# Layer 0 first, the modulation whole inside it, the context inside layer 1, its projections behind the attention part

## What is computed

```python
def first_block(x, p, positions, ...):                 # two layers
    cos, sin = rotary_tables(positions, x.dtype)
    h = x
    for i in range(DEPTH):                             # DEPTH = 2
        hn = rmsnorm(h, norm1[i])
        z = hn @ w_in[i]                               # pool part u, q, k, v
        ...                                            # rotary on q and k
        pool_out = pool_mixer(u, pool_w[i], pool_scale[i])
        attn_out = dilated_mixer(q, k, v)              # 12 heads of 64
        h = h + concat([pool_out, attn_out]) @ w_out[i]
        hn = rmsnorm(h, norm2[i])
        h = h + square(relu(hn @ w_up[i])) @ w_down[i] # 1024 -> 4096 -> 1024
        gate = sigmoid(rmsnorm(h, norm3[i]) @ w_gate[i])
        h = h + gate * (p[i] @ w_ple[i])
    return rmsnorm(h, final_norm)

def second_block(x, c, ctx, c_ctx, w_mod, b_mod, ...): # one layer
    mod = silu(c) @ w_mod + b_mod                      # w_mod is 1024 x 6144
    mod_c = silu(c_ctx) @ w_mod + b_mod
    ...
    h = modulate(x, norm1_g, sh1, sc1)
    hc = modulate(ctx, norm1_g, csh1, csc1)            # ctx: 256 context tokens
    ...
    # gated delta rule, 4 heads of 128, both directions: the context's final
    # state is the latent's first; of the context only k, v, beta and g count
    o_ctx, o_lat = bidir_gated_delta(dn_ctx, dn_lat)
    mix = branch_merge(h, o_lat, ...)                  # three branches and w_o
    x = x + g1 * mix
    x = x + g2 * swiglu(modulate(x, norm2_g, sh2, sc2), w_ffn_in, w_ffn_out)
    return rmsnorm(x, final_g)
```

## Time and profile before

| | |
|---|---|
| median of 3 runs | 1499.83 us |
| the profiled execution: its span, its own time | 1493.0 us, 1494.76 us |
| busy on PE, DVE, ACT, POOL | 1354.7, 902.5, 701.3, 134.1 us |
| prelude | 0 to 222.2 us |
| layer 0, layer 1 | 222.2 to 571.3 us, 574.2 to 929.8 us |
| latent part | 930 to 1493 us |
| read from HBM | 216.26 MB |

### The profile page before, as it was taken

The page is one execution under the profiler, slowest core; times in us unless marked ns, Lnnn a source line. Parts: engine busy times, 40 slices in busy tenths (PEclk is TensorE's granted clock), DMA queues, the critical chain, the costliest instruction groups (busy, mean ns, idle before and its releaser), DMA issues.

```text
span 1493.0 us, 26105 instructions
## 1 busy us (share of the span) xinstructions
PE 1354.7 (91%) x10476; PEld 1282.4 (86%) x10476; DVE 902.5 (60%) x1265; ACT 701.3 (47%) x1025; POOL 134.1 (9%) x110
## 2 busy tenths in 40 slices
PE   2896889979999988979999998898889999999997
PEld 2775779869999987968999998898778999899997
DVE  2867867755555467675555458756755556554553
ACT  3754544545444445464444445654424454534442
POOL 0025011120000010130000004001520000000000
PEclk9988999989999999979999999899999999999999
DMA  8742634325555553523555544344200555455550
GB/s 298 226 141 86 206 113 142 114 85 167 172 170 182 176 187 105 163 76 114 169 170 184 200 157 138 113 142 142 85 1 29 170 191 166 141 181 189 178 169 29
DMA packets 175843, 219.04 MB, mean 147 GB/s; under 512 B 5001, under 2 KB 159463, under 8 KB 175591
## 3 DMA queue, kind: packets, MB, share of 16 engines
q1 hardware_dynamic: 173986, 212.80, 43.8%
q10 hardware_dynamic: 1732, 4.52, 0.8%
HBM read 216.26 MB, written 1.05 MB: 146 GB/s over the span
## 4 chain that ended last, share of the span: by engine, by line
PE 74%; DVE 12%; DVEq 4%; issue 4%; ACT 3%; DMA 1%; ACTq 0%; SPq 0%
PE bank L629 21%; PE bank L631 20%; PE bank L630 20%; DVE w_lo L620 2%; PE bank L1359 2%; PE bank L870 1%; PE bank L858 1%; DMA w_raw<-in_w_mod 1%; DVE arena L1174 1%; ACT w_hi L611 1%; PE bank L1540 1%; PE bank L1422 1%; DVE arena L2200 1%; PE bank L1341 1%; DVEq L2160 1%
## 5 line engine op out<-in xcount | busy, mean ns | idle before, releaser
L620 DVE TENSOR_TENSOR w_lo<-w_raw,w_hi 128x1024 fp32r<-128x1024 f32 (+1 forms) x406 | 491.5, 1252 | 178.0 <-ACT w_hi L611 170.2
L629 PE MATMUL bank<-act_hi,w_hi 128*128 128x256 f32 x1808 | 522.0, 289 | 29.7 <-DVE act_lo L2123 11.1
L630 PE MATMUL bank<-act_lo,w_hi 128*128 128x256 f32 x1808 | 517.1, 286 | 0.0
L631 PE MATMUL bank<-act_hi,w_lo 128*128 128x256 f32 x1808 | 516.8, 286 | 0.0
L611 ACT ACTIVATE w_hi<-w_raw 128x1024 fp32r<-128x1024 f32 (+1 forms) x406 | 405.0, 1041 | 168.2 <-PE bank L631 112.8
L629 PEld LDWEIGHTS bank<-act_hi,w_hi 128*128 128x128 f32 x1808 | 352.8, 195 | 36.5 <-issue 12.7
L630 PEld LDWEIGHTS bank<-act_lo,w_hi 128*128 128x128 f32 x1808 | 352.8, 195 | 0.3 <-issue 0.2
L631 PEld LDWEIGHTS bank<-act_hi,w_lo 128*128 128x128 f32 x1808 | 352.6, 195 | 0.0
L629 PE MATMUL bank<-side_hi,w_hi 128*128 128x256 f32 x896 | 258.9, 289 | 6.7 <-DVE w_lo L620 6.7
L630 PE MATMUL bank<-side_lo,w_hi 128*128 128x256 f32 x896 | 254.8, 284 | 0.0
L631 PE MATMUL bank<-side_hi,w_lo 128*128 128x256 f32 x896 | 254.8, 284 | 0.0
(11 more groups left out here) (315 smaller groups left out, 1510.2 us busy)
## 6 DMA issues: line engine op xcount, KB each, us to landing
w_raw<-in_w_in SPq DMA_DIRECT2D x40, 1024.0 KB, 5.6
w_raw<-in_w_up SPq DMA_DIRECT2D x32, 1024.0 KB, 5.6
w_raw<-in_w_down SPq DMA_DIRECT2D x32, 1024.0 KB, 5.4
w_raw<-in_w_mod SPq DMA_DIRECT2D x24, 1024.0 KB, 5.2
w_raw<-in_w_ffn_in SPq DMA_DIRECT2D x22, 1024.0 KB, 5.1
w_raw<-in_w_gate SPq DMA_DIRECT2D x20, 1024.0 KB, 5.1
w_raw<-in_w_ffn_out SPq DMA_DIRECT2D x11, 1024.0 KB, 4.9
w_raw<-in_w_out SPq DMA_DIRECT2D x8, 1024.0 KB, 5.0
```

The costliest lines, as they stand in the source:

```text
L620: nc.vector.tensor_tensor(wlo[:, slot, 0:n], raw[:, l % RAW, n * half:n * (half + 1)], whi[:, slot, 0:n].bitcast(F32), ALU.subtract).then_ ...
L629: nc.tensor.matmul(o, ahi, bhi, start=start, stop=False, skip_group_check=True)
L630: nc.tensor.matmul(o, ahi, blo, start=False, stop=False, skip_group_check=True)
L631: return nc.tensor.matmul(o, alo, bhi, start=False, stop=stop, skip_group_check=True)
```

## The change

The prelude is gone, and the layers are written out one after the other instead of as a loop.

- Layer 0 starts as soon as the vectors and `x` are in. Its normed input is made straight from the PSUM banks with the transposed `x`.
- The modulation goes whole into layer 0. `w_mod` is cut in 24 chunks of 512 rows by 512 columns, and nothing is split: PE reads the loaded chunk itself as the fp32 moving operand, with 32 stationary columns (`mod_cond`, tile `silu_c_cols`, of which two hold numbers and the rest zeros). The four row tiles of a chunk write to four groups of 32 partitions of one bank. One pair of chunks fills a bank. ACT copies it (`modr`), `mod_columns` sums the groups and turns them into columns, and DVE adds the offsets (`modc`). Twelve chunks stand between the transposes and products of the attention part, twelve behind the down steps of the feed-forward part, one to every third step from step 16 on (`ATT_EXTRA`, `FFN_EXTRA`).
- The context goes into layer 1. ACT scales its rows in the q and k part, PE transposes them behind step 4, ACT makes the modulated `hc`. Behind the last V stand its four projections, unsplit too (`project_whole`: 16 fp32 matmuls of 256 columns a chunk), its `ba` product and the convolution. Then comes its delta rule, and 31 of layer 1's 36 steps from out0 on are put between its links, one at each of 31 places, by `FILL["ctx"]`.
- The stream of chunks has one order for all stages (class `Stream`). The slot of an unsplit chunk is free when PE has read it (`direct_done`), that of a split one when DVE has split it, as before.
- The last layer makes no normed input for a next layer any more. `cur_vec` and its copies at each layer's start are gone.
- In the delta rule `el` has two buffers, and for the context the key products (L1139 before) come behind the filler of their link.

```diff
-MOD_CHUNKS = 6 * D // 256
-MOD_FIRST = 2 * D // 256
-CTX_CHUNKS = 4
+MOD_PAIRS = 6 * D // 512
+MOD_CHUNKS = 2 * MOD_PAIRS
...
-FILL = {"ctx": dict(norm=2, tok=1, T3=1, z1=1, z2=1, z3=1, z4=1, z5=1, z6=1, x1=1, x2=1, x3=1, x4=1, x5=1, u0=1),
+FILL = {"ctx": dict(ba=1, norm=2, tok=1, T0=1, T1=1, T2=1, T3=1, P=1, x0=1, u1=1, u3=1, s0=1,
+                    **{f"{w}{lv}": 1 for w in "zxt" for lv in range(1, LEVELS)}),
...
+CTX_LAYER = 1
...
+ATT_EXTRA = (
+    {"v2": mod(0, 1, 2, 3), 0: [("modr", 0)] + mod(4, 5), 1: [("modr", 1), ("modc", 0)] + mod(6, 7),
+     2: [("modr", 2), ("modc", 1)] + mod(8, 9), 3: [("modr", 3), ("modc", 2)] + mod(10, 11),
+     4: [("modr", 4), ("modc", 3)], 5: [("modr", 5), ("modc", 4)], "V": [("modc", 5)]},
+    {"V": [("ctx", 0), ("ctx", 1), ("conv", 0), ("ctx", 2), ("conv", 1), ("ctx", 3), ("conv", 2), ("conv", 3), ("ba", 0)]})
+FFN_EXTRA = ({}, {})
+for j in range(6, MOD_PAIRS):
+    for at, entry in ((0, ("mod", 2 * j)), (2, ("mod", 2 * j + 1)), (3, ("modr", j)), (4, ("modc", j))):
+        FFN_EXTRA[0].setdefault(16 + 4 * (j - 6) + at, []).append(entry)
...
+            early = 8 if layer == 0 else 0
+            for s in range(LAYER_CHUNKS):
+                if s == 10:
+                    add_direct(direct[:early])
+                if s == (11 if layer == 0 else 12):
+                    add_direct(direct[early:])
+                st.add((layer, s), src[s], CH // 2 if s in (46, 47) else CH)
+                add_direct(FFN_EXTRA[layer].get(s - 1, []))
...
+        def project_whole(pe, name, bank, act):
+
+            pe.wait_ge(landed[st.slot(name)], st.loads(name))
+            for m in range(2):
+                for k in range(KT):
+                    at = 256 * k + P * m
+                    mm = nc.tensor.matmul(ps[bank][:, T * m:T * (m + 1)], raw[:, st.slot(name), at:at + P], act[:, k, :],
+                                          start=k == 0, stop=k == KT - 1)
+            mm.then_inc(direct_done, 1)
...
-            def mod_chunk():
...
-                o = ps[6 + m % 2][0:4, 0:256]
-                for half in range(2):
-                    slot = (2 * l + half) % PIECES
-                    pe.wait_ge(lo_ready, pre_w.pieces(l, half))
-                    for k in range(4):
-                        f = 4 * half + k
-                        for w in (whi, wlo):
-                            mm = nc.tensor.matmul(o, mod_in[:, f, :], w[:, slot, 256 * k:256 * (k + 1)],
-                                                  start=f == 0 and w is whi, stop=f == KT - 1 and w is wlo)
-                    mm.then_inc(pieces_done, 1)
...
+            def mod_columns(j):
+
+                b = banks.bank(f"mod{j}")
+                pe.wait_ge(S("mod_copied"), j + 1)
+                for i in range(4):
+                    mm = nc.tensor.matmul(ps[b][:, 2 * i:2 * i + 2], mod_rows[j % 4][:, P * i:P * (i + 1)],
+                                          col("mod_sum", 0, 2), start=True, stop=True)
+                full(mm, b)
+
+            def mod_chunk(i, take):
+
+                j, r = i // 2, i % 2
+                if r == 0:
+                    banks.claim(pe, f"mod{j}", take())
+                b = banks.bank(f"mod{j}")
+                name = ("mod", i)
+                if i == 0:
+                    pe.wait_ge(S("small_tables"), 1)
+                pe.wait_ge(landed[st.slot(name)], st.loads(name))
+                for k in range(4):
+                    mm = nc.tensor.matmul(ps[b][32 * k:32 * (k + 1), :], mod_cond[:, 4 * r + k, :],
+                                          raw[:, st.slot(name), 512 * k:512 * (k + 1)], start=r == 0, stop=r == 1,
+                                          skip_group_check=True)
+                mm.then_inc(direct_done, 1)
...
-            pe_delta(pe, "ctx", pre_w, MOD_FIRST, "pre", filler("ctx", mod_chunk))
-            for m in range(MOD_CHUNKS - 2, MOD_CHUNKS):
-                mod_columns(m)
-
-
-            with pe.Fori(0, DEPTH) as layer:
+            for layer in range(DEPTH):
...
+                    if s == 4 and layer == CTX_LAYER:
+                        features_first(lambda c: CL(f"ctx{c}"), in_tok,
+                                       lambda c: pe.wait_ge(S("ctx_scaled"), 1) if c == 0 else None)
...
+                    elif kind == "mod":
+                        mod_chunk(x, high)
+                    elif kind == "modc":
+                        mod_columns(x)
+                    elif kind == "ctx":
+                        if x == 0:
+                            pe.wait_ge(S("hc_ready"), 4)
+                        project_whole(pe, ("ctx", x), banks.claim(pe, f"ctx_c{x}", high()), hc)
+                    elif kind == "ba":
+                        ctx_beta_alpha(low)
...
+                if layer == CTX_LAYER:
+                    pe_delta(pe, "ctx", D_CTX, high, filler("ctx", step))
+                while todo:
+                    step()
...
-                        split_lo(dve, w, 11)
-                    wait("cat_hi", n + 1, 7)
+                        split_lo(dve, chunk(layer, 11 if layer == CTX_LAYER else 10))
+                    if n == 6 and layer != CTX_LAYER:
+                        split_lo(dve, chunk(layer, 11))
+                    n += 1
...
-                    norm_lo("n1", LV, range(2 * c, 2 * c + 2), in_hi, in_lo, KT)
+                    if layer + 1 < DEPTH:
+                        norm_lo("n1", LV, range(2 * c, 2 * c + 2), in_hi, in_lo, KT)
...
+                if layer == CTX_LAYER:
+                    pool_delta(pool, "ctx", D_CTX)
...
+            def slot_free(n):
+
+                if n < RAW:
+                    return
+                before = st.chunks[n - RAW][0]
+                if before in st.split:
+                    sp.wait_ge(lo_ready, st.pieces(before, 1))
+                else:
+                    sp.wait_ge(direct_done, st.direct[before] + 1)
```

1450 lines of the change are left out of this document (678 added, 772 removed).

## The result

The changed kernel took 1426.74 us, the median of 4 runs from 1425.36 to 1429.02, and the kernel before 1498.93 in the same comparison. The ratio is 0.952, with a 95% interval of 0.9492 to 0.9547. The profiled execution took 1425.36 us, with a span of 1423.5; the prediction's sum for the span was 1425.

A forecast was written before the change was run, and what follows sets the result against it. PE's own stream was taken to set the time. From the 1493.0 us span, -194.4, +21, +18.4, +98 (layer 1), -5, -4.5 and -1.5 gave 1425; adding 1.8 and 3 gave 1430 us, range 1404 to 1468.

The forecast's parts named there:

- The start: Start to layer 0's qk1: without the prelude, qk1 begins at 34 us instead of 228.4, -194.4, give or take 4.
- the half clock: Layer 0's first step, qk0: its first 4 us run at half clock, as at the prelude's first matmuls.
- The unsplit chunk: A w_mod chunk on PE: its four fp32 matmuls overlap fully, 0.86 plus 0.14 for starting, 1.0 us.
- rival A: Modulation chunks in layer 0: the column tiles run one after the other, +29 and +20, 1479 us; chance 0.12.
- The attention part: Layer 0, end of v2 to out0: ring and loads of 12 chunks stretch 24.7 to 45.5 us, +21 (+17 to +27).
- The feed-forward part: Layer 0, where PE is dense: 12 chunks at 1.0 and 6 mod_columns at 1.08 add 18.4 us.
- The projections: Layer 1, context: four fp32 projections take 27.3 us of PE and ba 3.4, less 1 of a covered wait.
- The weave: Layer 1, context's delta rule between steps: 48.2 us of its own matmuls and 16.3 of waits.
- B: Layer 1's steps between delta-rule links: w_lo comes 1 us late at each of 31 steps, +30, 1460; chance 0.14.
- D: Same steps: DVE's splits and PE's links run in turn, from 2.3 us a step, slower than before; chance 0.04.
- The turn of the loop: Before qk1 of layer 1: loop turn and issue vanish, with a 3.7 us gap on PE and some clock, -5.
- The dropped input: Before the latent part: the last layer's normed input, behind which DVE waited 2.88 us, goes, -4.5.

The follow-up runs named there:

- The quarter loads: Against the changed kernel, the 12 w_mod chunks of layer 0's attention part load 256 KB instead of 1 MB each; 1415.17 us.
- the added work: Changed kernel plus seven ACT copies and seven DVE subtractions into scratch beside each of the 24 unsplit w_mod chunks; 1458.98 us.
- The bare chain: Changed kernel with the context's FILL empty, so its delta rule runs by itself and the 36 steps follow; 1452.35 us.

## Why the prediction was right

- The start, -194.4, measured -196.8. The first step began 2.5 us sooner than I had put it. The likely reason is that the constants' load is the first one issued now, and that PE could start at 8.8 us rather than 13.3; no run tries the order of the loads alone. The price that I gave to the half clock was right: 8.2 us for qk0 against 6.0.
- The unsplit chunk, 1.0 us, measured 1.00 in the feed-forward part and 0.89 back to back. The step from two tiles side by side to four was an extrapolation, and a lucky one: the row that it started from, 0.88 us for 1.28 in series, is a gain of 1.45 and not of 2. The kernel with one tile shows that all of rival A's 49 us hung on it. The estimate of 1.2 that I had made from the Trainium skill's figure for three column tiles ("TensorE: Matmul & The Clock Gate", Measured speedup vs the span model) is above the measured 1.00, and the measurement decides. The Trainium skill's rule in "TensorEngine Tiling (Array Packing)", Key Properties, that a change of the tiling mode drains TensorE, fits the 0.11 us between 1.00 alone and 0.89 in a row, but no run tells that from an ordinary start.
- The attention part, +21, measured +23.6. The mechanism was the predicted one (four batches, chunk 11 behind out0's split, landed 35.5 us after v2 against 36). What is left of the miss lies behind chunk 11, 12.8 us where I had put 9. The quarter loads show that 10 us of the 23.6 hang on the size of the loads, and the added work that ACT and DVE have little to spare beside it.
- The feed-forward part, +18.4, measured +18.0. ACT's and DVE's part is hidden there: even the added work cost 1.6 us.
- The projections, 30.7, measured 31.2.
- The weave, 48.2 + 16.3, measured 62.6, of which the waits are 12.8 and PE's own part 49.8. Two of the waits were read from the order and are in the trace: 6.80 for 5.7 and 5.13 for 5.4. The place of the second was right, its size was in part luck: 3.84 for the sum of squares, 1.4 for the key products, 1.28 and 1.93 for POOL, less 5.75 of cover, is 2.7 and not 5.4. In the trace the sum of squares starts 2.9 us behind the start of the step that is to cover it, since the pair of relu operations with its waits for ACT stands ahead of it, and this is what the written sum leaves out. The small waits were too large (2.7 for the vt bank was 0.73). The 48.2 is a slip of 0.3, since 41.7 and 6.8 are 48.5. Rivals B and D fall: no steady link waits, so there is no wait that repeats 31 times. The bare chain shows how little there was to hide: of its 89 us PE works 67, part of it at the lower clock, and the 31 steps hide 25.6, under 1 us at each place.
- The turn of the loop, -5, measured -3.9: the gap of 3.7 is gone, and the clock that I had added to it gave 0.2 and not 1.3.
- The dropped input, -4.5: too large. The place gave 2.5 and the latent part, which I had put at nothing, another 1.2; put back, the input costs 3.2 over both.
- From the span to the median of the runs I had added 1.8 and 3. It was 1.8 and 1.4, so the forecast of 1430 is 3.3 over 1426.74, about half by the sum and half by this.

The terms' errors, from -2.4 to +2.6, cancelled to 1.5 us in the sum. So the sum is better than its terms, and part of that is luck. The range was wide for rivals A and B, not for the terms.

## What to carry to other kernels

Price moved work by the stage that takes it, from its rows: a pair of unsplit chunks cost 3.0 us where PE was dense and 3.9 in the stretch that looked empty, because there the ring of slots and a split on another engine set the order of the loads. For a skinny operand, four column tiles in place of one were worth 50 us here, and reading the chunk unsplit keeps ACT and DVE out of a path where added work cost up to 29. A wait for a bank that was taken away came back at the next claim of a bank, 4.97 of 6.80 us, since the one who frees it came no sooner. And before a difference of 2 or 3 us is put down to an edit, look at the same stage in runs that do not touch it.
